# A two-block network on one core: state-space stage reordered, keys up-projected by head pairs, tokens and output moved in pieces

## The reference

```
q  = (rms_norm(cq, q_norm) @ w_q_up).reshape(B, S, 8, 96)          # 64 plain + 32 rotary per head
kv = (rms_norm(ckv, kv_norm) @ w_kv_up).reshape(B, S, 8, 64 + 64)  # keys and values
...
bu = einsum('blgc,gpc->blgp', u, bb)              # complex: 64 groups of 16 inputs, 64 states each
x  = associative_scan(complex_scan_op, (a, bu))   # x[t] = a * x[t-1] + bu[t]
y  = real(einsum('blgp,gcp->blgc', x, c)) + d_skip * u
g  = gelu(y)
ga, gb = split(g @ w_glu, 2)
return ga * sigmoid(gb)
```

## Time and profile before

| | us |
|---|---|
| median of three runs | 1734.09 (1732.87 to 1734.72) |
| the profiled execution | 1734.25 |
| its span | 1732.5 |
| PE busy | 1680.5, 97% of the span |
| DVE, ACT, POOL busy | 780.0, 312.6, 58.7 |
| mean granted TensorE clock | 0.991 of full |

### The profile page before, as it was taken

One profiled execution on the slowest core, in us unless ns is written; L12 is line 12 of the kernel. 1 busy time (PEld: TensorE's weight loads), 2 busy tenths in 40 slices (PEclk: granted clock), 3 DMA queues, 4 the chain that ended last, 5 costly groups with the idle time before them and its releaser, 6 DMA issues.

```text
span 1732.5 us, 23056 instructions
## 1 busy us (share of the span) xinstructions
PE 1680.5 (97%) x9354; PEld 1422.2 (82%) x9354; DVE 780.0 (45%) x1686; ACT 312.6 (18%) x686; POOL 58.7 (3%) x84
## 2 busy tenths in 40 slices
PE   7999999999999999999999999999999898999998
PEld 6758888888888868888888785788888787788887
DVE  6645354323365414654345576466542272433310
ACT  2131210000052102100001323322220121122200
POOL 0000000000000000290000000000000000000000
PEclk9999999999999999999999999999999899999999
DMA  6445468875654664766554232244435303444455
GB/s 221 128 136 172 152 235 306 289 241 190 211 170 160 225 223 140 249 219 224 181 166 147 85 121 97 91 141 153 151 123 170 122 3 101 140 149 157 148 162 177
DMA packets 78297, 289.23 MB, mean 167 GB/s; under 512 B 8688, under 2 KB 8688, under 8 KB 77424
## 3 DMA queue, kind: packets, MB, share of 16 engines
q1 hardware_dynamic: 78192, 287.76, 49.3%
HBM read 286.67 MB, written 1.05 MB: 166 GB/s over the span
## 4 chain that ended last, share of the span: by engine, by line
PE 93%; DVE 5%; issue 1%; ACT 1%; DMA 0%; SPq 0%; DVEq 0%; ACTq 0%
PE acc L380 71%; PE acc L449 5%; PE acc L435 3%; PE acc L944 3%; PE acc L390 1%; PE acc L560 1%; PE score L584 1%; PE score L540 1%; PE score L650 1%; PE score L896 1%; PE acc L611 1%; DMA ring<-stream 0%; PE turned L595 0%; PE acc L871 0%; PE acc L910 0%
## 5 line engine op out<-in xcount | busy, mean ns | idle before, releaser
L380 PE MATMUL acc<-H,ring 128*128 128x256 f32 x3528 | 770.2, 380 | 7.3 <-DVE H L1451 3.0
L380 PEld LDWEIGHTS acc<-H,ring 128*128 128x128 f32 x3528 | 667.0, 190 | 108.7 <-issue 11.5
L380 PE MATMUL acc<-FFN,ring 128*128 128x256 f32 x1408 | 306.5, 381 | 0.0
L380 PEld LDWEIGHTS acc<-FFN,ring 128*128 128x128 f32 x1408 | 268.5, 191 | 37.3 <-issue 0.4
L380 PE MATMUL acc<-big,ring 128*128 128x256 f32 x880 | 192.1, 379 | 0.9 <-PE acc L380 0.9
L380 PEld LDWEIGHTS acc<-big,ring 128*128 128x128 f32 x880 | 166.9, 190 | 24.6 <-issue 2.0
L1608 DVE SCALAR_TENSOR_TENSOR bT<-bT,cond 128x1024 f32<-128x1024 f32 x58 | 75.7, 1305 | 77.8 <-DMA bT<-ada_in 74.1
L1803 DVE SCALAR_TENSOR_TENSOR pair<-acc,cols,pair 128x255 f32<-128x255 f32 x84 | 40.5, 482 | 121.1 <-ACT pair L1121 117.9
L1466 DVE TENSOR_TENSOR X<-acc,X 128x256 f32<-128x256 f32 x48 | 20.4, 425 | 147.7 <-PE acc L380 138.7
L1468 DVE SCALAR_TENSOR_TENSOR X<-acc,mod,X 128x256 f32<-128x256 f32 x24 | 11.6, 484 | 148.4 <-PE acc L380 145.0
L1121 ACT ACTIVATE pair<-acc,cols 128x256 f32<-128x256 f32 x84 | 47.2, 564 | 161.7 <-PE acc L380 161.7
(11 more groups left out here) (411 smaller groups left out, 1366.8 us busy)
## 6 DMA issues: line engine op xcount, KB each, us to landing
ring<-stream SPq DMA_DIRECT2D x440, 512.0 KB, 3.5
bT<-ada_in SPq DMA_DIRECT2D x70, 512.0 KB, 4.5
big<-ada_in SPq DMA_DIRECT2D x26, 512.0 KB, 4.4
big<-ssm_in SPq DMA_DIRECT2D x2, 1024.0 KB, 5.7
cols<-cols_in SPq DMA_DIRECT2D x1, 1169.5 KB, 7.2
X<-x_in SPq DMA_DIRECT2D x1, 1024.0 KB, 4.8
MEM<-mem_in SPq DMA_DIRECT2D x1, 1024.0 KB, 12.2
y_out<-X SPq DMA_DIRECT2D x1, 1024.0 KB, 3.9
```

The lines of the kernel that those rows point to most:

```text
L380: mm = nc.tensor.matmul(dst, w[:, k * cols_per:(k + 1) * cols_per], r, start=first and n == 0, stop=last and n == len(src) - 1)
```

## The change

Five edits.
- SP issues 16 columns of the table, two quarters of the tokens, slot 0, the other two quarters, slot 1, and the rest of the table. The engines wait for the piece that they use; ACT squares by quarters and applies its first Silu after the first root.
- In `q_up` ACT copies the plain half of each head; DVE's final addition waits for it.
- `kv_up` makes the keys of two heads with one product into 128 rows; ACT copies each half by itself.
- In the state-space stage TensorE issues driven products and selects earlier; ACT issues all shifts ahead of moves 2 to 7, and the decays of tile n + 2 ahead of the gelu of tile n; parts of the first two gated tiles stand between the last read-outs.
- The output is stored tile by tile.

```diff
 STAGES = [
-    ("ev_in", 8, 8), ("xk0", 8, 8), ("q_up", 2, 8), ("xv0", 4, 2), ("kv_up", 1, 10), ("pool", 1, 4), ("xv0b", 4, 2),
+    ("ev_in", 8, 8), ("xk0", 8, 8), ("q_up", 2, 8), ("xv0", 4, 2), ("kv_up", 1, 6), ("pool", 1, 4), ("xv0b", 4, 2),
     ("att0", 0, 4),
...
 NCOLS = _n
+FIRST_COLS = 16
...
         params_in = sem("params_in")
+        gains_in = sem("gains_in")
+        x_loaded = [sem(f"x_loaded{i}") for i in range(4)]
         mem_loaded = sem("mem_loaded")
...
         pooled_done = sem("pooled_done")
+        q_copied = sem("q_copied")
         beside_out = sem("beside_out")
...
         def _(sp):
-            sp.dma_start(X[:], x_in).then_inc(params_in, 16)
-            sp.dma_start(cols[:], cols_in).then_inc(params_in, 16)
+            def tokens_in(i):
+                sp.dma_start(X[:, 512 * i:512 * i + 512], x_in[:, 512 * i:512 * i + 512]).then_inc(x_loaded[i], 16)
+            sp.dma_start(cols[:, 0:FIRST_COLS], cols_in[:, 0:FIRST_COLS]).then_inc(gains_in, 16)
+            tokens_in(0)
+            tokens_in(1)
             ada = 0
...
                 sp.dma_start(ring[s % RING][:], stream[s]).then_inc(loaded[s % RING], 16)
+                if s == 0:
+                    tokens_in(2)
+                    tokens_in(3)
+                if s == 1:
+                    sp.dma_start(cols[:, FIRST_COLS:], cols_in[:, FIRST_COLS:]).then_inc(params_in, 16)
                 while ada < N_ADA and ADA_AFTER[ada] == s:
...
                     sp.dma_start(V, ssm_in[1]).then_inc(c_in, 16)
-            sp.wait_ge(acc_free, 4 + TILE0["down3"] + 8)
-            sp.dma_start(out, X[:]).then_inc(stored, 16)
-            sp.wait_ge(stored, 16)
+            for k in range(KD):
+                sp.wait_ge(acc_free, 4 + TILE0["down3"] + k + 1)
+                sp.dma_start(out[:, k * S:(k + 1) * S], at(X, k)).then_inc(stored, 16)
+            sp.wait_ge(stored, 16 * KD)
...
             pe.sem_inc(acc_free, 4)
-            pe.wait_ge(params_in, 32)
             pe.wait_ge(ones_set, 1)
...
             w = slot_in("kv_up", 0)
-            for h in range(MLA_H):
-                t = TILE0["kv_up"] + h
+            for p in range(MLA_H // 2):
+                t = TILE0["kv_up"] + p
                 bank_free(t)
-                product(acc[t % 4][0:NOPE, 0:S], w[:, h * NOPE:(h + 1) * NOPE], [at(H, 2)], NOPE).then_inc(part_done, 1)
+                product(acc[t % 4][:, 0:S], w[:, p * P:(p + 1) * P], [at(H, 2)]).then_inc(part_done, 1)
             for b in range(2):
-                t = TILE0["kv_up"] + MLA_H + b
+                t = TILE0["kv_up"] + MLA_H // 2 + b
                 bank_free(t)
...
                                  start=True, stop=True).then_inc(part_done, 1)
-            end_parts(10)
+            end_parts(6)
             w = slot_in("pool", 0)
...
             pe.wait_ge(s5_kernels_out, 1)
+            def gated(k, first, last):
+                w = slot_in("glu", k)
+                if first == 0:
+                    bank_free(TILE0["glu"] + k)
+                for n in range(first, last):
+                    i = S5_ORDER[n]
+                    if k < 2:
+                        pe.wait_ge(s5_gelu, n + 1)
+                    mm = nc.tensor.matmul(acc[(TILE0["glu"] + k) % 4][:, 0:S], w[:, i * P:(i + 1) * P], at(MEM, i),
+                                          start=n == 0, stop=n == KD - 1)
+                if last == KD:
+                    mm.then_inc(slot_used, 1)
             select(0)
...
             select(2)
+            select(3)
+            driven(1)
             local(0)
-            driven(1)
-            select(3)
             select(4)
+            select(5)
             local(1)
             driven(2)
-            select(5)
             select(6)
...
                 read_out(n)
-                if 3 <= n + 2 < KD:
-                    driven(n + 2)
+                if n + 3 < KD:
+                    driven(n + 3)
                 if n + 4 < KD:
                     local(n + 4)
-            for k in range(16):
-                w = slot_in("glu", k)
-                bank_free(TILE0["glu"] + k)
-                for n, i in enumerate(S5_ORDER):
-                    if k == 0:
-                        pe.wait_ge(s5_gelu, n + 1)
-                    mm = nc.tensor.matmul(acc[(TILE0["glu"] + k) % 4][:, 0:S], w[:, i * P:(i + 1) * P], at(MEM, i),
-                                          start=n == 0, stop=n == KD - 1)
-                mm.then_inc(slot_used, 1)
+                if n == KD - 3:
+                    gated(0, 0, 5)
+                if n == KD - 2:
+                    gated(0, 5, 6)
+                    gated(1, 0, 6)
+            gated(0, 6, 8)
+            gated(1, 6, 8)
+            for k in range(2, 16):
+                gated(k, 0, KD)
             up("up3", lead([("up3", 0), ("up3", 1)], gained_in_ffn, S + 1))
...
-            act.wait_ge(params_in, 32)
+            for i in range(4):
+                act.wait_ge(x_loaded[i], 16)
+                ins = nc.scalar.activation(at(SQ, 2 * i, 2), at(X, 2 * i, 2), ACT.Square)
+            ins.then_inc(norm_squares, 1)
+            norms[0] += 1
+            inputs[0] += 1
+            act.wait_ge(norm_vars, 1)
+            nc.scalar.activation(root[:], variance[:], ACT.Sqrt).then_inc(norm_rstd, 1)
+            act.wait_ge(params_in, 16)
             nc.scalar.activation(cond[:], col("c", 0, 8), ACT.Silu).then_inc(cond_done, 1)
-            norm(X, KD)
             act.wait_ge(mem_loaded, 16)
...
             squares(6, 1)
+            for h in range(MLA_H):
+                act.wait_ge(part_done, PARTS0["q_up"] + h + 1)
+                nc.scalar.activation(at(Q, h, lo=0, hi=NOPE), acc[(TILE0["q_up"] + h) % 4][0:NOPE, 0:S], ACT.Copy)\
+                    .then_inc(q_copied, 1)
             variance_root()
...
             values("xv0", V0, 0)
-            for h in range(MLA_H):
-                act.wait_ge(part_done, PARTS0["kv_up"] + h + 1)
-                nc.scalar.activation(at(K, h, lo=0, hi=NOPE), acc[(TILE0["kv_up"] + h) % 4][0:NOPE, 0:S], ACT.Copy)\
-                    .then_inc(acc_free, 1)
+            for p in range(MLA_H // 2):
+                act.wait_ge(part_done, PARTS0["kv_up"] + p + 1)
+                for e in range(2):
+                    ins = nc.scalar.activation(at(K, 2 * p + e, lo=0, hi=NOPE),
+                                               acc[(TILE0["kv_up"] + p) % 4][NOPE * e:NOPE * e + NOPE, 0:S], ACT.Copy)
+                ins.then_inc(acc_free, 1)
             for b in range(2):
-                act.wait_ge(part_done, PARTS0["kv_up"] + MLA_H + b + 1)
-                nc.scalar.activation(V[:, b * D:b * D + 512], acc[(TILE0["kv_up"] + MLA_H + b) % 4][:, :], ACT.Copy)\
+                act.wait_ge(part_done, PARTS0["kv_up"] + MLA_H // 2 + b + 1)
+                nc.scalar.activation(V[:, b * D:b * D + 512], acc[(TILE0["kv_up"] + MLA_H // 2 + b) % 4][:, :], ACT.Copy)\
                     .then_inc(acc_free, 1)
...
                     act.wait_ge(s5_state, n - 1)
                 nc.scalar.activation(at(probs, 2 * (n % 2), 2).rearrange("p (e q c) -> p e q c", e=2, c=CHUNKS)[:, :, :, 1:CHUNKS],
...
             shifted(0)
-            for n in range(1, KD):
+            shifted(1)
+            moved(0)
+            shifted(2)
+            moved(1)
+            for n in range(3, KD):
                 shifted(n)
-                moved(n - 1)
-            moved(KD - 1)
+            for n in range(2, KD):
+                moved(n)
             begin("s5")
...
                 i, t = S5_ORDER[n], TILE0["s5"] + n
+                if n + 2 < KD:
+                    decays(n + 2)
                 act.wait_ge(s5_y, n + 1)
...
                 act.sem_inc(acc_free, 1)
-                if n + 2 < KD:
-                    decays(n + 2)
             begin("glu")
...
             dve.sem_inc(ffn_mid, 2)
-            dve.wait_ge(params_in, 32)
+            dve.wait_ge(gains_in, 16)
...
             for k in range(KD):
+                if k % 2 == 0:
+                    dve.wait_ge(x_loaded[k // 2], 16)
                 ins = v.tensor_scalar(gained_in_ffn(k), at(X, k), col("ev_norm", k), None, ALU.mult).then_inc(gained, 1)
...
             lead_norm(gained_in_ffn, rstd[:])
+            dve.wait_ge(params_in, 16)
             begin("ev_in")
...
                 dve.wait_ge(part_done, PARTS0["q_up"] + h + 1)
-                v.tensor_copy(at(Q, h, lo=0, hi=NOPE), b[0:NOPE, 0:S])
                 own(v.tensor_tensor(pair[NOPE:96, 2 * S:3 * S], b[NOPE:96, 0:S], c0, ALU.mult))
                 own(v.tensor_tensor(pair[NOPE:96, 3 * S:4 * S], b[96:128, 0:S], s0, ALU.mult))
+                dve.wait_ge(q_copied, h + 1)
                 v.tensor_tensor(at(Q, h, lo=NOPE, hi=96), pair[NOPE:96, 2 * S:3 * S], pair[NOPE:96, 3 * S:4 * S], ALU.add)\
...
```

## The result

The changed kernel takes 1718.08 us (median of four runs, 1717.19 to 1719.17) against 1734.07 us, a ratio of 0.9911 with a 95% interval of 0.9899 to 0.9923: faster by 16.0 us, where 21.35 were forecast. It lies inside the range. The profiled execution took 1717.98 us around a span of 1716.2.

A forecast was written before the change was run, and what follows sets the result against it. TensorE, busy 97% of the span, was taken as the bound. Gains 3.5 + 2.6 + 1.8 + 0.85 + 10.8 + 1.8 = 21.35 us off 1734.25 gave 1712.9, stated as 1713.0; range 1710.5 to 1720.0.

The forecast's parts named there:

- rival (a): State-space stage gives half: read-out 0 wait grows or clock stays low; 5.4 us less gain, 1718.4 us; 13%.
- The start: First loads: slot 0 lands at 5.9, sums of squares start at 9.8 instead of 13.3; gain 3.5 us, bounds 1.5 and 4.3.
- Rival (c): Start: requests in flight share the engines, so slot 0 lands with the table as before; 1716.5 us; 10%.
- rival (b): Clock falls before the values as before and stays low for eight more instructions at the start; 1.8 + 1.7 us, 1716.5; 12%.
- Queries, clock, keys: Attention: ACT's head copies gain 2.6 us, clock staying up at the values 1.8, paired keys 0.85.
- The stage: State-space stage: earlier shifts, decays and driven products remove three DVE waits; gain 10.8 us, ends 7.5 and 11.5.
- The clock rises within 1388 to 1389: State-space stage: TensorE's clock reaches its full level between 1388 and 1389 us, used to price the new order.
- TensorE needs 5.05 us per tile, just less than DVE: State-space stage: TensorE takes 5.05 us a tile against DVE's 5.50.
- The stores: Output by tiles: eighth store issued 0.4 us late at 1728.5, landing at 1730.3; gain 1.8 us, between 0.9 and 2.3.
- The store being the nearer row: Stores: non-data part of a store taken as 1.5 us, from the 1 MB store's 1.4 rather than a slot load's 2.3.
- Rival (d): Stores and start: a queue serves one request at a time, each paying its fixed part; slower, 1739.7 us; 3%.
- milder form: Stores and start: one request at a time at 1.8 us a store; sum 1731.5 us, no change; 2%.

The follow-up runs named there:

- run 1: The changed kernel with the old start alone (tokens and whole table, one request each, one wait): 1716.94 us, ratio 0.9909.
- run 8: The changed kernel with tokens in one request behind the small table piece, and stores of four, three and one tile: 1714.65 us, ratio 0.9895.
- run 10: The changed kernel with twelve unread products before the stage, three stores, and whole tokens first, the small table piece behind them: 1708.98 us, ratio 0.986.
- run 2: The changed kernel with the old query and key parts (DVE copies, keys head by head): 1723.71 us, ratio 0.9943.
- run 9: The changed kernel with the old order of the state-space stage and twelve unread products ahead of it: 1722.69 us, ratio 0.9938.
- run 6: The changed kernel with twelve unread products before the stage and read-out 0 ahead of selects 6, 7 and locals 2, 3: 1712.08 us, ratio 0.988.
- runs 5: The changed kernel with twelve unread products on TensorE in its wait ahead of the state-space stage: 1711.37 us, ratio 0.9874.
- run 11: Like run 10, with sixteen more unread products on TensorE while the first data come: 1709.24 us, ratio 0.986.
- run 7: The changed kernel with twelve unread products before the stage and all gated products behind the last read-out: 1718.13 us, ratio 0.991.

## Why the prediction was right, and where it was wrong

**The total.** 16.0 us were gained of 21.35, and the time lies in the range because the range was wide and the misses went one way: 2.2 us at the start, 1.7 at the stores and 1.2 in the stage. That it falls next to rival (a)'s 1718.4 is chance, since only 1.2 of (a)'s 5.4 us came. The clock's part is luck too. With the low stretch of runs 1 and 8 (6.8 us in place of 17.1) the stage would take some 54.1 us and the kernel some 1713.7, by estimate: next to the forecast of 1713.0, with the start and the stores as wrong as they are.

**The start** (3.5 forecast, 1.26 measured, below the lower bound of 1.5). The step that failed is that the small piece, half of the tokens and slot 0, 1.06 MB in all, would be through when 1.05 MB were through before, so that slot 0 lands at 5.9 with "0.4 us because four requests at 0.54 replace one". That takes the byte rate of one set of requests for another. Tokens by pieces move in rows of 2 KB, behind a piece of 64 B rows, and the rate from 2.25 to 4.5 us was 96 to 208 GB/s. By the rates, 1.06 MB are through at some 4.8 us before, at 5.0 with the tokens whole and first (run 10), at 5.3 with the small piece ahead of them (run 8), and at 6.35 with small piece and quarters. So about 0.3 us go to the place of the small piece and about 1.0 to the quarters, by one profile each. Rival (c), which shared this outcome, had the wrong mechanism: requests were served in order, only slower. 0.8 us more went to the low clock in the sums, the first half of what rival (b) said. The clock came up at 13.13 us before, 0.2 us ahead of the sums, and at 12.67 in the middle of them after; in run 1, with the old start, it came up at 15.36, behind them. So this part was luck of the profile before, and not the edit.

**Queries, clock, keys** (2.6, 1.8 and 0.85; measured 2.58, 1.60 and 0.77). The steps held: 1.37 us a head, ACT in time, and a pool bound by DVE 15.24 us behind the variance. That the clock stays up was the uncertain one; run 2 brings the idle time and the low clock back together, and makes this part 6.2 us, as its low stretch was the longer one. The conclusion was right, but its ground was weak: it was read from an idle time of 2.0 us from 1398 on that left the clock at 1.00. The same wait, 2.21 us for ACT at local 4, is followed by the low clock in run 9.

**The stage** (10.8; 9.58). The order laid out by hand held to the release: read-outs every 5.03 us, the three waits gone, the table load for gelu 0 taken at 1391.34 ahead of read-out 0 and free. What failed is "The clock rises within 1388 to 1389", taken over from the profile before: the clock's rise was taken as fixed to the work, and it isn't. In the seven profiles without unread products ahead, before and after among them, it was low around the first select for 17.1 us three times, 13.7 once and 6.8 three times. Rival (a) named a clock that stays low in the stage, at half of the gain; it cost 1.2 us. Its other half, a growing wait on read-out 0, did come (1.88 us for 1.4), but TensorE had no idle time behind it, and run 6 gives the order of read-out 0 0.44 us. And "TensorE needs 5.05 us per tile, just less than DVE" understates what TensorE does: all of the stage's 58.4 us are its own work, so any of its clock counts in full.

**The stores** (1.8; 0.14). Two terms were too small: the eighth request comes out 0.8 us behind the update (0.4), since an issue takes 0.50 and not 0.45 us and eight stand in one row; and its landing takes 3.0 us, not 1.8. Behind a single store of 384 KB still in flight, the same 128 KB land in 2.3 us (run 8) and 2.5 (run 10). The forecast gave the eighth store an empty queue, but the last slot's 0.52 MB and the 1.05 MB of all the stores are issued within 4.4 us and move up to 1715, 3 us behind the update. "The store being the nearer row", a 1 MB store's part that isn't data, was the wrong choice; the slot's load with 2.3 was nearer. By the Trainium skill (DMA: Bandwidth & Descriptors, Bandwidth) requests should be batched; for eight stores against three the runs agree, for one against three they don't, since what counts is how much is still to be moved at the last update: 4.76 us with one, 4.68 to 5.19 with eight, 3.23 to 3.36 with three. The 6.15 us of that page are for a load that GpSimd issues; for this store they were no estimate, and its row has 3.9.

**Rival (d)**, one request at a time, is out: the eight stores land within 6.6 us of the first issue. Its milder form was worked out wrongly: at 1.8 us a store, 1.5 of them fixed, the same steps give 7.6 us at the stores and 2.7 at the start, so some 1728.5 and not 1731.5. Not in the forecast was that the long middle differs by itself: 0.34 us less, with one stretch of 6.8 us at the low clock after, and two of 3.4 before, at places that nothing edited.

## What to carry to other kernels

Look at the granted clock in front of every stage of many small matmuls: where TensorE waits there for a norm, put unread products into the wait, and judge a new order with the clock up, since otherwise its gain is mixed with chance (12.3 us became 9.6). A shorter wait can be worth more than its length: 0.86 us less idle time kept the clock up. Where the bounding engine waits at the end of a stage for another engine's last steps, begin the next stage's work there (4.8 us). Let the first request be large with long rows (shown for this start alone), and send the finished part of the output early, so that one small store is left behind the last result.

## What the runs showed of the hardware

- The same instructions at the same place run at the low clock for different lengths: around the first select 17.1, 6.8 or 13.7 us, and elsewhere 3.4 or 6.8, or none. With it the stage in the new order goes from 54.06 to 59.44 us. In runs 5, 6, 10 and 11, with unread products ahead and the new order, the clock stayed up through the stage, and it took 52.96, 52.52, 52.77 and 52.79 us. In run 7 it fell inside, where TensorE waited for DVE, and in run 9 twice, once where it waited for ACT and once for DVE.
- At the start TensorE needs 3.75 us for eight instructions of 256 columns, although the profile gives a granted clock of 1.00; with sixteen products ahead, 2.00. The trace's first record of the clock comes when the matmuls become fast, at 12.67 us in the change and at 4.75 in run 11.
- Requests behind one another are cheap in issue (0.43 to 0.50 us on SP) and dear in landing: 128 KB take 2.3 to 2.5 us behind one store of 384 KB in flight and 3.0 to 3.9 in a row of eight.
- The first packets of a run are slow: those of 8 KB that start within the first 2 us take 0.80 us on average before and 1.01 in run 10, and 0.31 from 3 us on. Packets of 2 KB in the change take 0.17 us between 2 and 3 us and 0.09 from 6 us on.
